# Two attention blocks and two plain MLP entries: output-projection parts and transposes of x at other places in TensorE's order

## The reference

```python
h = h + merge_heads(mix) @ w_o[layer]                       # residual
h = h + squared_relu_mlp(rms_norm(h, mlp_norm[layer]), w_up[layer], w_down[layer])
```

## Time and profile before

| | before |
|---|---|
| median of three runs | 1212.42 us |
| the profiled execution | 1212.66 us |
| its span on the core | 1211.0 us |
| TensorE (PE) busy | 1180.5 us, 97% |
| VectorE (DVE) busy | 838.8 us, 69% |
| ScalarE (ACT) busy | 598.1 us, 49% |
| HBM read | 234.37 MB, 194 GB/s over the span |

### The profile page before, as it was taken

The page is one execution under the profiler, slowest core; times in us unless marked ns, Lnnn a source line. Parts: engine busy times, 40 slices in busy tenths (PEclk is TensorE's granted clock), DMA queues, the critical chain, the costliest instruction groups (busy, mean ns, idle before and its releaser), DMA issues.

```text
span 1211.0 us, 19661 instructions
## 1 busy us (share of the span) xinstructions
PE 1180.5 (97%) x7827; PEld 1072.5 (89%) x7827; DVE 838.8 (69%) x1127; ACT 598.1 (49%) x791; POOL 73.6 (6%) x111
## 2 busy tenths in 40 slices
PE   8999999999999999999999999999999999999997
PEld 8897899999889789999989999998988888999996
DVE  6676798888866669888576654457986866544545
ACT  5545544444545554444465334346756756434343
POOL 9200011110000001110000000000000000000000
PEclk9999999999999999999999999999999999999999
DMA  7633598997453259987635655544651053656560
GB/s 252 225 115 102 212 366 307 322 313 276 132 196 126 70 209 343 322 308 279 203 107 185 199 187 195 173 150 157 192 193 51 31 198 120 209 176 197 172 202 35
DMA packets 143241, 236.38 MB, mean 195 GB/s; under 512 B 6358, under 2 KB 106951, under 8 KB 143175
## 3 DMA queue, kind: packets, MB, share of 16 engines
q1 hardware_dynamic: 130402, 196.73, 48.8%
q0 software_dynamic: 10400, 37.77, 8.6%
q10 hardware_dynamic: 2372, 0.96, 0.3%
HBM read 234.37 MB, written 1.05 MB: 194 GB/s over the span
## 4 chain that ended last, share of the span: by engine, by line
PE 92%; DVE 4%; ACT 2%; issue 1%; POOL 0%; DVEq 0%; ACTq 0%; POOLq 0%
PE ps L1839 13%; PE ps L1841 13%; PE ps L1840 13%; PE ps L1949 10%; PE ps L1951 10%; PE ps L1953 10%; PE ps L1886 2%; PE ps L1888 2%; PE ps L1887 2%; PE ps L2038 1%; PE ps L2040 1%; PE ps L2039 1%; PE ps L2120 1%; PE ps L1973 1%; PE ps L1913 1%
## 5 line engine op out<-in xcount | busy, mean ns | idle before, releaser
L1065 DVE TENSOR_TENSOR wlo<-raw,whi 128x2048 fp32r<-128x2048 f32 (+2 forms) x185 | 417.3, 2260 | 194.3 <-ACT whi L610 193.9
L610 ACT ACTIVATE whi<-raw 128x2048 fp32r<-128x2048 f32 (+2 forms) x185 | 348.6, 1887 | 230.4 <-PE ps L1953 128.4
L1839 PE MATMUL ps<-ah,whi 128*128 128x256 f32 x1296 | 367.2, 283 | 3.3 <-DVE wlo L1538 1.4
L1840 PE MATMUL ps<-al,whi 128*128 128x256 f32 x1296 | 366.7, 283 | 0.0
L1841 PE MATMUL ps<-ah,wlo 128*128 128x256 f32 x1296 | 366.7, 283 | 0.0
L1839 PEld LDWEIGHTS ps<-ah,whi 128*128 128x128 f32 x1296 | 248.5, 192 | 6.2 <-DVE wlo L1538 1.7
L1840 PEld LDWEIGHTS ps<-al,whi 128*128 128x128 f32 x1296 | 248.6, 192 | 1.8
L1841 PEld LDWEIGHTS ps<-ah,wlo 128*128 128x128 f32 x1296 | 248.6, 192 | 0.0
L1949 PE MATMUL ps<-whi,hh 128*128 128x512 f32 x376 | 116.6, 391 | 0.0
L1951 PE MATMUL ps<-wlo,hh 128*128 128x512 f32 x376 | 116.1, 390 | 0.0
L1953 PE MATMUL ps<-whi,hl 128*128 128x512 f32 x376 | 116.0, 390 | 0.0
(11 more groups left out here) (415 smaller groups left out, 1788.6 us busy)
## 6 DMA issues: line engine op xcount, KB each, us to landing
stage<-in_w_ada_dram POOLq DMA_DIRECT2D x72, 512.0 KB, 6.7
raw<-in_w_up_dram SPq DMA_DIRECT2D x32, 1024.0 KB, 6.4
raw<-in_w_down_dram SPq DMA_DIRECT2D x32, 1024.0 KB, 7.5
raw<-in_ffn_w_gate_dram SPq DMA_DIRECT2D x22, 1024.0 KB, 5.3
raw<-in_ffn_w_up_dram SPq DMA_DIRECT2D x22, 1024.0 KB, 5.3
raw<-in_ffn_w_down_dram SPq DMA_DIRECT2D x22, 1024.0 KB, 5.0
raw<-in_moba_w_qkv_dram SPq DMA_DIRECT2D x11, 1024.0 KB, 7.4
raw<-in_w_in_dram SPq DMA_DIRECT2D x10, 1024.0 KB, 5.2
```

Source lines behind the costliest of these rows:

```text
L610: A.activation(whi[:, s, 0:size], raw[:, s, 0:size], ACT.Copy).then_inc(w_hi, 1)
L1065: V.tensor_tensor(wlo[:, s, 0:size], raw[:, s, 0:size], whi[:, s, 0:size].bitcast(F32), ALU.subtract).then_inc(w_lo, 1)
L1839: T.matmul(o, wmh, xh[:, c], start=(c == 0), stop=False)
L1840: T.matmul(o, wmh, xl[:, c], start=False, stop=False)
```

## The change

TensorE's head loop from head 10 on: weights_T(10) and the first part of the output projection (c = 0, t = 1, bank 7) come ahead of score(12); part (0, 0) comes after it. VectorE runs normalise(10) ahead of the last `qk_copy` instead of behind it. After weights_T(15) the first part of unit n0+13 comes ahead of the last `values`. In `wo_units` 12 of the 16 transposes of x (all of t = 0, and c = 0 to 3 of t = 1) come ahead of the last group (1,1); the other four come inside `entry_unit`, after 9 of its 48 matmuls. ScalarE and VectorE treat pairs 0 and 1 ahead of the last part of the residual, ScalarE ahead of the split of unit U_MLP+1 too. The number of matmuls and of transposes stays the same. The diff, cut to its core (layer 1's lines repeat those of layer 0):

```diff
-        FIRST_WO = [[(0, 0), (0, 1)], [(1, 0)], [(1, 1)], [(2, 0), (2, 1)], [(3, 0)], [(3, 1)]]
+        FIRST_WO = [[(0, 0)], [(1, 0)], [(1, 1)], [(2, 0), (2, 1)], [(3, 0)], [(3, 1)]]
...
# ScalarE
             block_heads(U_ATT0, 0, 0)
+            splits(U_MLP0)
+            gained("mlp0", ah, col(vA, COL_A, "mlp_norm"), npairs=2, bank_of=O_BANK)
             splits(U_MLP0 + 1)
-            gained("mlp0", ah, col(vA, COL_A, "mlp_norm"), bank_of=O_BANK)
+            gained("mlp0", ah, col(vA, COL_A, "mlp_norm"), first=2, bank_of=O_BANK)
...
# VectorE, block_heads
                 for h in range(H):
+                    if h < WOVEN:
+                        normalise(h + 1)
                     if h == WOVEN - 1:
                         qk_copy(n0, 3 + h // 2)
-                    if h < WOVEN:
-                        normalise(h + 1)
...
# VectorE; residual(idx, t, v) is now one part
+            def residual_entry(idx, stage_name, gain):
+                for t, v in ((0, 0), (0, 1), (1, 0)):
+                    residual(idx, t, v)
+                gained(stage_name, ah, al, gain, npairs=2, bank_of=O_BANK)
+                residual(idx, 1, 1)
+                gained(stage_name, ah, al, gain, first=2, bank_of=O_BANK)
...
             splits(U_MLP0)
-            residual(0)
-            gained("mlp0", ah, al, gcol("mlp_norm"), bank_of=O_BANK)
+            residual_entry(0, "mlp0", gcol("mlp_norm"))
             splits(U_MLP0 + 1)
...
# TensorE, block_heads
                     else:
+                        if h == WOVEN:
+                            weights_T(h)
+                            unit_wait(n0 + 12)
+                            pe.wait_ge(in_ready, PAIR0[stage_name] + 1)
+                            wo_part(n0 + 12, 1, 0, 0, True, False)
                         if h + 2 < H:
                             score(h + 2)
                         for c, t in FIRST_WO[h - WOVEN]:
-                            if c == 0 and t == 0:
-                                unit_wait(n0 + 12)
...
-                        weights_T(h)
+                        if h > WOVEN:
+                            weights_T(h)
+                        if h == H - 1:
+                            unit_wait(n0 + 13)
+                            wo_part(n0 + 13, 0, 1, 0, True, False)
...
+            def early_T(j):
+                for t in range(TT):
+                    for c in range(CT - 4 * t):
+                        if c == 0:
+                            pe.wait_ge(x_half, TT * (j - 1) + t + 1)
+                        elif c == 4:
+                            pe.wait_ge(x_ready, TT * (j - 1) + t + 1)
+                        ins = T.transpose(ps[:, O_BANK[c // 2], (c % 2) * S + t * P:(c % 2) * S + (t + 1) * P],
+                                          x[:, t, c * P:(c + 1) * P], ident[:])
+                        if t == 1 and c % 2 == 1:
+                            ins.then_inc(tr_done, 1)
+
+            def late_T(j):
+                pe.wait_ge(x_ready, TT * j)
+                for c in range(4, CT):
+                    ins = T.transpose(ps[:, O_BANK[c // 2], (c % 2) * S + P:(c % 2) * S + 2 * P],
+                                      x[:, 1, c * P:(c + 1) * P], ident[:])
+                    if c % 2 == 1:
+                        ins.then_inc(tr_done, 1)
...
# TensorE, wo_units
                 for t in range(TT):
                     for v in range(2):
                         if t == 0:
                             unit_wait(n0 + 2 + v)
+                        if t == 1 and v == 1:
+                            early_T(j)
                         for c in range(4, 8):
...
# TensorE, mlp: entry_unit calls within() at (c, m) == (1, 1)
-                entry_unit(n0, slot(n0), 4, ah, al, stage_name)
+                entry_unit(n0, slot(n0), 4, ah, al, stage_name, within=lambda: late_T(1 if n0 == U_MLP0 else 3))
...
-            wo_units(U_WO0, "o0")
-            raw_T(1, bank_of=O_BANK)
+            wo_units(U_WO0, "o0", 1)
```

More of the change, by code:

```diff
@@ L919, in _ @@
             block_heads(U_ATT1, H, 1)
+            splits(U_MLP1)
+            gained("mlp1", ah, col(vA, COL_A, "mlp_norm", CT), npairs=2, bank_of=O_BANK)
             splits(U_MLP1 + 1)
-            gained("mlp1", ah, col(vA, COL_A, "mlp_norm", CT), bank_of=O_BANK)
+            gained("mlp1", ah, col(vA, COL_A, "mlp_norm", CT), first=2, bank_of=O_BANK)
             square(3)
@@ L1277, in part_wait, with residual @@
                     dve.wait_ge(half_done, HALF0[idx] + 2 * t + v + 1)
[L1279 to L1287, removed]
+            def residual(idx, t, v):
+                if t == 0:
+                    dve.wait_ge(half_done, HALF0[idx] + v + 1)
+                else:
+                    dve.wait_ge(w_used, RES_END[idx] - 1 + v)
+                xv = x[:, t, v * 512:v * 512 + 512]
+                V.tensor_tensor(xv, xv, bank(WO_BANK[t][v]), ALU.add).then_inc(x_ready if v else x_half, 1)
+            def residual_entry(idx, stage_name, gain):
[4 more added lines that the diff above has]
+                gained(stage_name, ah, al, gain, first=2, bank_of=O_BANK)
             def scaled_residual_halves(idx, k):
@@ L1595, in _ @@
             splits(U_MLP1)
-            residual(2)
-            gained("mlp1", ah, al, gcol("mlp_norm", CT), bank_of=O_BANK)
+            residual_entry(2, "mlp1", gcol("mlp_norm", CT))
             splits(U_MLP1 + 1)
@@ L2146, in gate_rows, with wo_units @@
                 ins.then_inc(gate_ps, 1)
-            def wo_units(n0, stage_name):
-                unit_wait(n0 + 1)
+            def early_T(j):
[16 more added lines that the diff above has]
+                        ins.then_inc(tr_done, 1)
+            def wo_units(n0, stage_name, j):
                 for c in range(4):
                     for t in range(TT):
-                        ins = wo_part(n0 + 1, t, 1, c, c == 0, False)
+                        if (c, t) != (0, 0):
+                            ins = wo_part(n0 + 1, t, 1, c, c == 0, False)
                 ins.then_inc(w_used, 1)
@@ L2285, in _ @@
             block_heads(U_ATT1, H, 1, "o1", bh, bl)
-            wo_units(U_WO1, "o1")
-            raw_T(3, bank_of=O_BANK)
+            wo_units(U_WO1, "o1", 3)
             mlp(U_MLP1, CHUNK0["mlp1"], "mlp1", ADA0, ADA1)
```

## The result

The changed kernel takes 1207.76 us (median of 6 runs, 1207.04 to 1207.80); the profiled execution 1207.77, its span 1206.1. The forecast was 1207.6 and 1206.2. The ratio of that comparison to the kernel before is 0.9948 (0.9923 to 0.9974), a gain of 6.3 us; one of the six runs of the kernel before took 1222.26 us where the other five took 1212.23 to 1212.72, and it counts in the ratio. Timed again, with 11 runs beside 35 of the kernel before, the ratio is 0.9961 (0.9942 to 0.9981), and the medians are 1207.65 and 1212.57: 4.92 us.

The account below looks back on a forecast made before the run. TensorE, 92% of the chain that ended last, was taken as the bound, so only its idle time could go. 0.9 + 0.70 + 0.79 = 2.39 us per layer, 4.8 for both, gave 1207.6 us; range 1206.5 to 1209.5.

Parts of the forecast that it names:

- Head 12: Ahead of score(12): weights_T(10) and one part fill TensorE's wait for `qk_copy`; gain 0.9 us per layer, 0.6 to 1.0.
- Last values: Ahead of the last `values`: one part fills TensorE's wait for ScalarE's copy; gain 0.70 us per layer, 0.6 to 0.73.
- Entry, TensorE: MLP entry: TensorE's 1.28 us wait for `al` goes; the entry ends 1.20 us earlier per layer.
- Entry, VectorE: Behind the MLP entry: VectorE's split makes the first `d_unit` wait 0.35 us; 0.79 of 1.20 us remain per layer.
- A: MLP entry: pair 2 is 0.8 us late, the entry gains nothing; 1209.2 us; chance 0.13 together with E.
- B: Ahead of score(12): the gap only moves to score(13) or weights_T(11); gain 3.0 us, time 1209.4; chance 0.08.
- C: Behind the MLP entry: VectorE does not bind, for example because pair 2 is earlier; gain 5.8 us, time 1206.6; chance 0.09.
- E: Ahead of the last group: the 12 transposes wait uncovered for x, residual(1,0) over 1.2 us late; A's time; 0.13 with A.
- D: Last group and entry: TensorE's clock falls to 1.2 of 2.4 GHz; 6.9 us slower, 1219.3; chance 0.04.
- changes of kind in TensorE's stream: About four added per layer, 0.1 + 0.08 us charged; charging all costs 0.2 more per layer, the skill's rule makes them free.

Follow-up runs that it names:

- entry only: Kernel before with only the transposes around the last group and in the entry, plus the matching ScalarE and VectorE order: 1210.96 us.
- head 12 only: Kernel before with only weights_T(10) and one part ahead of score(12), normalise(10) ahead of the last `qk_copy`: 1210.50 us.
- `norm_sq` behind the body: Changed kernel with VectorE's `norm_sq` moved from ahead of the MLP to behind its whole first body: 1206.86 us.

## Why the prediction was right or wrong

The mechanism came as forecast: three waits gone, one new one at the first `d_unit`, and a sum of 4.8 us against 4.92. What failed is the step from this sum to the range. The prediction says that a measurement of this kernel tells 0.2% (2.4 us) from no change, and its range of 1206.5 to 1209.5 us is put together from the rivals alone; the error of the comparison is put at nothing. What it had to go by were three runs of the kernel before, which lay within 0.43 us. The comparison then had an interval of 0.9923 to 0.9974, which is 6.2 us wide, and its centre, 0.9948 of 1212.42 us, is 1206.1 us, below the range, while the median of the changed kernel, 1207.76, lies inside it. The cause is the one run of 1222.26 us: the other five of the kernel before have a mean of 1212.54, the six of the changed kernel 1207.64, a ratio of 0.9960 and 4.9 us; timed again the ratio is 0.9961, and the spans (1211.0 and 1206.1) differ by 4.9 us. The forecast's own range is wrong as well: it is given as 1207.0 to 1208.3 "from the bounds of the terms", but these bounds (0.6 to 1.0, 0.6 to 0.73, 0.5 to 1.20 per layer) add up to gains of 3.4 to 5.9 us, thus some 1206.6 to 1209.0.

Some terms of the sum were mis-sized too, by up to 0.14 us per layer, and their errors cancel; that the sum is right to 0.1 us is in part luck. Per layer, step by step (forecast, then measured by the part alone in layer 0 and 1):

- **Head 12**: 0.9, measured 1.04 and 1.00, at and above the bound of 1.0. score(12) starts at 99.83 (forecast 99.85), normalise(10) at 97.02 (97.1), score(13) at 102.21 (102.3). My charge of 0.10 for entering `values` from a part was right (101.08 + 0.23 = 101.31, against 101.41). A score cost 0.79 (99.83 to 100.62) where I had counted 0.85, from a score that stood right behind a wait, and the 0.94 of my working went into the sum as 0.9.
- **Last values**: 0.70, measured 0.66 and 0.60. A part nearly fits in the gap: `values` starts 1.12 us after weights_T(15), where it was 1.06 in the earlier trace rows and forecast as 1.03. The missing 0.1 is the entry into `values` from a part (112.92 to 113.25, 0.33 for 0.23): I charged it at head 12 and put it at nothing here.
- **Entry, TensorE**: 1.20, of which 0.06 lost at the next unit. The 12 transposes take 1.35 (127.11 to 128.46; forecast 1.48): at 0.109 each that is 1.31, so of the forecast wait of 0.17 for residual(1,0) at most 0.04 are there. The group behind them gives that back: it takes 2.85 where 2.72 was forecast. The late ones start 5.27 us after the early ones (5.35) and cost 0.36 (0.44), and `a_unit` starts 10.48 after the early ones (10.61). Before it was 11.75 from the same mark (128.77 to 140.52), so 1.27 us are gained up to here, 0.13 more than forecast.
- **Entry, VectorE**: the new wait at the first `d_unit` was forecast as 0.35; it is there, 143.78 against some 143.4. What remains of the entry is 0.84 and 0.80 against 0.79. The forecast counted the chain split, `norm_sq`, L1420, L1423, split as 8.4 us from 136.97; it is 8.38 (135.25 to 143.63). That it binds is shown by taking `norm_sq` out of it.
- **Rivals**: A (entry given back) is out by "entry only"; B (gap moves) by "head 12 only"; C (VectorE doesn't bind) by `norm_sq` behind the body, which gains the 0.35 per layer that C would have had for nothing; E by the timeline (12 transposes in 1.35). D: in the changed kernel the granted clock is 1.00 in each stretch of 5 us from 115 to 150 us, where group and entry lie. As to changes of kind in TensorE's stream, the first matmul behind transposes takes 0.31 to the next (112.38 to 112.69) where one in the stream takes 0.23, and the last of a part takes 0.33 to `values`, so each costs 0.08 to 0.1. The Trainium skill ("TensorE: Matmul & The Clock Gate", "What happens when you issue a matmul") says that a matmul's drain lies under the next one's fill; that such changes are therefore free, as the prediction drew from it, does not hold here.

## What to carry to other kernels

When one engine bounds, list its waits, and for each write down when every partner of the moved instruction is done, in the order of that partner's own queue; here one swap on VectorE (normalise ahead of `qk_copy`) decides between 1.0 us gained and 0.6 us lost per layer. Charge the same price at every place where the same two instructions meet. A gain at one wait ends where the next engine's chain begins: follow that chain to the first instruction that TensorE takes from it, and move what nobody waits for yet (13 small instructions, needed only at the end of the MLP) to a place with more room than it takes. The gains of the three separate parts added up here to 0.01 us. A forecast of a measured time has two errors, that of the sum and that of the comparison; the second belongs in the range too.

## What the runs showed of the hardware

TensorE's granted clock can fall to half for some 20 us with the same program. In the profiled execution of "head 12 only", which took 1218.16 us where the median of that kernel is 1210.50, it does so between 945 and 970 us, in the second block's hybrid mixer, which the change does not touch (it is the number before the last two in these rows of stretches; before it stand start and end, then the busy times of the engines):

```profile
940.00:945.00 5.00, 4.85 (x42) 4.71 (x40) 4.57 (x9) 4.88 (x15) 0.00 (x0) 1.00 0.00 0
945.00:950.00 5.00, 4.46 (x26) 4.19 (x27) 3.50 (x9) 3.54 (x11) 0.00 (x0) 0.82 0.00 0
950.00:955.00 5.00, 5.00 (x25) 5.00 (x24) 1.55 (x3) 2.19 (x6) 0.00 (x0) 0.50 0.01 3
...
965.00:970.00 5.00, 5.00 (x20) 4.36 (x20) 4.30 (x2) 4.81 (x4) 0.00 (x0) 0.64 0.14 26
```

0.50 is 1.2 of 2.4 GHz. From 925 to 950 us, up to the fall, TensorE was busy for 4.46 to 5.00 of each 5 us; in the profiled execution of the kernel before, a stretch with as little (4.26 in 955 to 960) kept 1.00. What tips it is open. Of the 165 executions on record for all kernels, 14 took some 8 to 10 us more than the median of their kernel; the 13 of them whose mean granted clock is on record have 0.989, all others on record 0.997 to 0.999. The 1222.26 us in the first comparison is the one without a recorded clock, so that its clock fell is likely and not shown.
